# A macaron block on one core: the residual stream is laid out token by partition

## The reference, cut to what matters

```
h = rms_norm(x, g_ffn1_pre)
x = x + 0.5 * rms_norm((silu(h @ w_gate) * (h @ w_up)) @ w_down, g_ffn1_post)      # d_ff = 4096

h = rms_norm(x, g_mix_pre);  proj = h @ w_in      # q,k,v (8 heads x 64), q,k,v,g (4 x 128), two gates (1024 each)
o_sb = stick_breaking_attention(q_sb, k_sb, v_sb)              # strictly causal
o_r  = group_norm(retention(rotary(q_r), rotary(k_r), v_r)) * silu(g_r)
merged = sigmoid(gate_sb) * (o_sb @ w_proj_sb) + sigmoid(gate_ret) * (o_r @ w_proj_ret)
x = x + rms_norm(merged @ w_out, g_mix_post)

h = rms_norm(x, g_ffn2_pre)                                    # then a second FFN like the first
```

## Time and profile before

| | |
|---|---|
| three runs | 1584.85, 1585.07, 1587.95 us |
| span of the profiled execution | 1583.4 us; the page gives no time of its own for that execution beyond the span |
| TensorE busy | 1535.9 us (97%) |
| VectorE, ScalarE, GpSimd busy | 638.3, 495.1, 96.5 us |
| DMA | 138.67 MB, 88 GB/s over the span |
| chain that ended last | PE 93%, DVE 5%, ACT 1%, DMA 1% |

### The profile page before, as it was taken

One profiled execution on the slowest core, in us unless ns is written; L12 is line 12 of the kernel. 1 busy time (PEld: TensorE's weight loads), 2 busy tenths in 40 slices (PEclk: granted clock), 3 DMA queues, 4 the chain that ended last, 5 costly groups with the idle time before them and its releaser, 6 DMA issues.

```text
span 1583.4 us, 17821 instructions
## 1 busy us (share of the span) xinstructions
PE 1535.9 (97%) x6549; PEld 1213.2 (77%) x6549; DVE 638.3 (40%) x753; ACT 495.1 (31%) x689; POOL 96.5 (6%) x145
## 2 busy tenths in 40 slices
PE   6999999999999979999999999899999999999996
PEld 5888888888888767666657887678888888888884
DVE  4433333333333473435545444463333333333334
ACT  4312212222222343445554232332212222222222
POOL 1000000000000040321220000220000000000001
PEclk9999999999999979999999999899999999999997
DMA  6333333333222212111112334133333333322211
GB/s 208 94 106 93 93 106 93 93 102 107 95 93 93 79 53 82 53 53 54 34 34 68 99 86 133 54 93 93 93 101 93 98 94 93 117 94 93 93 40 54
DMA packets 201007, 138.67 MB, mean 88 GB/s; under 512 B 4448, under 2 KB 188816, under 8 KB 200848
## 3 DMA queue, kind: packets, MB, share of 16 engines
q1 hardware_dynamic: 200160, 135.28, 28.7%
q10 hardware_dynamic: 816, 2.98, 0.5%
HBM read 136.14 MB, written 2.10 MB: 87 GB/s over the span
## 4 chain that ended last, share of the span: by engine, by line
PE 93%; DVE 5%; ACT 1%; DMA 1%; issue 0%; ACTq 0%; POOL 0%; DVEq 0%
PE ps L378 28%; PE ps L379 28%; PE ps L380 28%; PE ps L578 2%; DVE h_lo L916 1%; PE ps L555 1%; DVE ys L911 1%; PE ps L503 1%; PE ps L505 1%; PE ps L504 1%; PE ps L542 1%; PE ps L559 1%; PE ps L546 1%; DVE acc L943 1%; DVE w_lo L888 1%; DMA x_tok<-x 1%
## 5 line engine op out<-in xcount | busy, mean ns | idle before, releaser
L378 PE MATMUL ps<-h_hi,w_hi 128*128 128x512 f32 x1312 | 525.0, 400 | 9.7 <-DVE h_lo L916 7.3
L380 PE MATMUL ps<-h_hi,w_lo 128*128 128x512 f32 x1312 | 512.5, 391 | 0.0
L379 PE MATMUL ps<-h_lo,w_hi 128*128 128x512 f32 x1312 | 512.5, 391 | 0.0
L888 DVE TENSOR_TENSOR w_lo<-w_raw,w_hi 128x1024 fp32r<-128x1024 f32 (+1 forms) x260 | 311.4, 1200 | 172.3 <-ACT w_hi L655 164.1
L378 PEld LDWEIGHTS ps<-h_hi,w_hi 128*128 128x128 f32 x1312 | 247.3, 188 | 79.9 <-issue 24.7
L379 PEld LDWEIGHTS ps<-h_lo,w_hi 128*128 128x128 f32 x1312 | 247.4, 189 | 53.0 <-issue 3.4
L380 PEld LDWEIGHTS ps<-h_hi,w_lo 128*128 128x128 f32 x1312 | 247.2, 188 | 52.5
L655 ACT ACTIVATE w_hi<-w_raw 128x1024 fp32r<-128x1024 f32 (+1 forms) x260 | 257.6, 1019 | 32.5 <-PE ps L380 25.2
L380 PE MATMUL ps<-a_hi,w_lo 128*128 128x512 f32 x512 | 202.2, 395 | 0.0
L378 PE MATMUL ps<-a_hi,w_hi 128*128 128x512 f32 x512 | 202.2, 395 | 0.0
L379 PE MATMUL ps<-a_lo,w_hi 128*128 128x512 f32 x512 | 202.2, 395 | 0.0
(11 more groups left out here) (140 smaller groups left out, 998.4 us busy)
## 6 DMA issues: line engine op xcount, KB each, us to landing
w_raw<-w_ffn_gate SPq DMA_DIRECT2D x64, 512.0 KB, 4.0
w_raw<-w_ffn_up SPq DMA_DIRECT2D x64, 512.0 KB, 4.0
w_raw<-w_ffn_down SPq DMA_DIRECT2D x64, 512.0 KB, 3.3
w_raw<-w_in SPq DMA_DIRECT2D x44, 512.0 KB, 3.8
w_raw<-w_out SPq DMA_DIRECT2D x8, 512.0 KB, 3.7
w_raw<-w_proj_sb SPq DMA_DIRECT2D x8, 256.0 KB, 2.6
w_raw<-w_proj_ret SPq DMA_DIRECT2D x8, 256.0 KB, 2.5
out<-x_tok SPq DMA_DIRECT2D x8, 256.0 KB, 2.7
```

The lines of the kernel that those rows point to most:

```text
L378: pe.matmul(ps[:, bank, :], wh, src_hi, start=first, stop=False)
L379: pe.matmul(ps[:, bank, :], wh, src_lo, start=False, stop=False)
L380: return pe.matmul(ps[:, bank, :], wl, src_hi, start=False, stop=last)
L888: dve.tensor_tensor(w_lo[:, slot, 0:cols], w_raw[:, slot, 0:cols], w_hi[:, slot, 0:cols].bitcast(F32), ALU.subtract).then_inc(w_lo_done, 1)
```

## The change

The residual stream is kept as `x_tok`, tokens on partitions (4 tiles, t, of 128 tokens by 1024 features). Each product that is added to it (down, out) is computed with the activations stationary and the weights moving (`row_product`), so a token tile's output is a pair of PSUM banks. Norms are sums along the free axis: ScalarE squares with `accum_out`, a root, a reciprocal on VectorE, and the scale and the gain (loaded broadcast to all partitions, `g_b`) are applied in one operation. h is normalised completely in `xn`, transposed by eight TensorE transposes a tile into PSUM and split to `h_hi` and `h_lo`; so the scaling by `r_all` is gone from the up projections, fills and merge, GpSimd's residual and squares are gone, and so are the transposes at the end. The last four units (`LAST = SLOTS`) of each down projection and of the out projection run token tile by token tile; at the two starts of an FFN the first four up units run in halves of 256 tokens. x and the first tables are loaded in another order.

Core of the diff (same on both FFNs and with like orders on each engine):

```diff
-        a_hi, e = place("a_hi", [P, 2, T], F32R, at=e)
+        a_hi, e = place("a_hi", [P, SLOTS, T], F32R, at=e)
...
+            def row_product(bank, s_hi, s_lo, slot, col, first, last):
+                wh, wl = w_hi[:, slot, col:col + T], w_lo[:, slot, col:col + T]
+                pe.matmul(ps[:, bank, :], s_hi, wh, start=first, stop=False)
+                pe.matmul(ps[:, bank, :], s_hi, wl, start=False, stop=False)
+                return pe.matmul(ps[:, bank, :], s_lo, wh, start=False, stop=last)
...
+            def transposed(n, t):
+                pe.wait_ge(xn_done, TT * n + t + 1)
+                for k in range(KD):
+                    mm = pe.transpose(ps[:, 2 * t + k // 4, tok(k % 4)], xn[:, t % 2, k * P:(k + 1) * P], c(IDENT))
+                mm.then_inc(xt_done, 1)
+            def half_unit(u, j, half):
+                if half == 0:
+                    pe.wait_ge(w_lo_done, u + j + 1)
+                cs = slice(half * 2 * P, (half + 1) * 2 * P)
+                for k in range(KD):
+                    mm = product(j, (j, k * P), h_hi[:, k, cs], h_lo[:, k, cs], k == 0, k == KD - 1, cs)
...
+            def last_down(fi, u0, t):
+                for f in range(NF - LAST, NF):
+                    if t == 0:
+                        pe.wait_ge(w_lo_done, f + u0 + 2 * NF + 1)
+                        pe.wait_ge(a_lo_done, f + NF * fi + 1)
+                    slot = f % SLOTS
+                    for dh in range(2):
+                        mm = row_product(2 * t + dh, a_hi[:, slot, tok(t)], a_lo[:, slot, tok(t)], slot, dh * T, ...)
...
+            last_down(0, U_UP1, 0)          # TensorE, FFN1 to mixing
+            last_down(0, U_UP1, 1)
+            last_down(0, U_UP1, 2)
+            transposed(1, 0)
+            last_down(0, U_UP1, 3)
+            transposed(1, 1)
+            values_sb(0)
+            transposed(1, 2)
+            values_sb(1)
+            transposed(1, 3)
+            values_sb(2)
+            values_sb(3)
...
+            last_out(0)                     # TensorE, mixing to FFN2
+            last_out(1)
+            last_out(2)
+            transposed(2, 0)
+            last_out(3, (0,))
+            transposed(2, 1)
+            last_out(3, (1,))
+            transposed(2, 2)
+            pe.wait_ge(h_lo_done, 2 * TT + 2)
+            half_unit(U_UP2, 0, 0)
+            half_unit(U_UP2, 1, 0)
+            half_unit(U_UP2, 2, 0)
+            transposed(2, 3)
+            half_unit(U_UP2, 3, 0)
+            pe.wait_ge(h_lo_done, 3 * TT)
+            for j in range(4):
+                half_unit(U_UP2, j, 1)
...
+            def y_spread(n, t, last_unit):      # ScalarE; x_spread is the same on x_tok
+                act_eng.activation(junk[:, :], bank_pair(t).rearrange("p b c -> p (b c)"), ACT.Square,
+                                   accum_out=ssq[:, t:t + 1]).then_inc(y_squared, 1)
+                act_eng.wait_ge(y_squared, TT * n + t + 1)
+                act_eng.activation(std[:, t:t + 1], ssq[:, t:t + 1], ACT.Sqrt, bias=cst[:, EPS:EPS + 1], scale=1.0 / D
+                                   ).then_inc(y_std, 1)
...
+            def into_stream(n, t, g, gain_half, halves=1):      # VectorE
+                dve.wait_ge(y_std, TT * n + t + 1)
+                dve.reciprocal(rstd[:, t:t + 1], std[:, t:t + 1]).then_inc(y_rstd, 1)
+                dve.wait_ge(y_rstd, TT * n + t + 1)
+                w = D // halves
+                for i in range(halves):
+                    cs = slice(i * w, (i + 1) * w)
+                    yv = bank_pair(t).rearrange("p b c -> p (b c)")[:, cs]
+                    dve.scalar_tensor_tensor(out=yv, in0=yv, scalar=rstd[:, t:t + 1], in1=g_b[:, G_SLOT[g], cs], ...)
+                    dve.wait_ge(y_scaled, TT * n + t + i + 1)
+                    dve.scalar_tensor_tensor(out=x_tok[:, t, cs], in0=yv, scalar=gain_half, in1=x_tok[:, t, cs], ...)
+            def normalise(n, t, g):
+                ...
+                dve.scalar_tensor_tensor(out=xn[:, t % 2, :], in0=x_tok[:, t, :], scalar=rstd[:, TT + t:TT + t + 1],
+                                         in1=g_b[:, G_SLOT[g], :], op0=ALU.mult, op1=ALU.mult).then_inc(xn_done, 1)
...
+            into_stream(0, 0, G_POST1, 0.5)     # VectorE, FFN1 to mixing
+            normalise(1, 0, G_PRE_MIX)
+            into_stream(0, 1, G_POST1, 0.5)
+            normalise(1, 1, G_PRE_MIX)
+            into_stream(0, 2, G_POST1, 0.5)
+            stream_lo(1, 0)
+            split_u(U_V)
+            normalise(1, 2, G_PRE_MIX)
+            split_u(U_V + 1)
+            split_u(U_V + 2)
+            split_u(U_V + 3)
+            into_stream(0, 3, G_POST1, 0.5)
+            stream_lo(1, 1)
+            normalise(1, 3, G_PRE_MIX)
+            stream_lo(1, 2)
+            stream_lo(1, 3)
...
-                        act_eng.wait_ge(q_scaled, 2 * s + j + 1)
+                        act_eng.wait_ge(unit_done, U_HEADS + f + 1)
```

More of the change, by code:

```diff
@@ L382, in unit @@
-            def unit(u, slot, bank, hi, lo, nk=KD, each_k=None, midway=None):
+                pe.matmul(ps[:, bank, out_cols], wh, src_hi, start=first, stop=False)
+                pe.matmul(ps[:, bank, out_cols], wh, src_lo, start=False, stop=False)
+                return pe.matmul(ps[:, bank, out_cols], wl, src_hi, start=False, stop=last)
+            def row_product(bank, s_hi, s_lo, slot, col, first, last):
[3 more added lines that the diff above has]
+                return pe.matmul(ps[:, bank, :], s_lo, wh, start=False, stop=last)
@@ L384, in unit @@
+            def unit(u, slot, bank, hi, lo, nk=KD):
                 pe.wait_ge(w_lo_done, u + 1)
                 for k in range(nk):
-                    if each_k is not None:
-                        pe.wait_ge(each_k[0], each_k[1] + k + 1)
-                    if midway is not None and k == nk // 2:
-                        midway()
                     last = product(bank, (slot, k * P), hi[:, k, :], lo[:, k, :], k == 0, k == nk - 1)
                 last.then_inc(unit_done, 1)
-            def token_sums(bank, squares, first, last):
-                for j in range(TT):
-                    mm = pe.matmul(ps[:, bank, j:j + 1], squares[:, j * P:(j + 1) * P], c(ONES, 1),
-                                   start=(first and j == 0), stop=last, skip_group_check=True)
-                return mm
@@ L446, in ffn, with down, step @@
                         up(i, j)
-                def down(f, slot, banks, first=False, last=False):
-                    pe.wait_ge(w_lo_done, f + u0 + 2 * NF + 1)
+            def down(fi, u0):
+                ud = u0 + 2 * NF
+                def step(f, slot, tiles=range(TT), first=False):
+                    pe.wait_ge(w_lo_done, f + ud + 1)
                     pe.wait_ge(a_lo_done, f + NF * fi + 1)
-                    for d in banks:
-                        if first and d == 0:
+                    for t in tiles:
+                        if first and t == 0:
@@ L458, in down @@
                     mm.then_inc(unit_done, 1)
-                pe.wait_ge(r_all_ready, 4 * fi + 1)
-                down(0, 0, (4, 5, 6, 7, 0, 1, 2, 3), first=True)
-                with pe.Fori(0, (NF - 3) // SLOTS) as turn:
+                step(0, 0, (2, 3, 0, 1), True)
+                with pe.Fori(0, (NF - SLOTS) // SLOTS - 1) as turn:
                     i = turn * SLOTS + 1
                     for j in range(SLOTS):
-                        down(i + j, (j + 1) % SLOTS, range(KD))
-                for f in range(NF - 3, NF):
-                    down(f, f % SLOTS, Y_ORDER, last=(f == NF - 1))
@@ new lines, in _, with copy_v @@
+            stream_hi(1, 1)
+            x_spread(1, 3)
+            stream_hi(1, 2)
+            stream_hi(1, 3)
+            def copy_v(n, dst, t, bank):
+                if t < TT - 1:
+                    act_eng.wait_ge(v_ready, (TT - 1) * n + t + 1)
+                else:
+                    act_eng.wait_ge(unit_done, U_V + 4 * n + 4)
+                act_eng.activation(dst[:, t, :], ps[:, bank, :], ACT.Copy).then_inc(v_copied, 1)
+            copy_v(0, v_sb, 1, 2)
+            for j in range(4):
+                split_u(U_V + 4 + j)
@@ L1029, in _ @@
[L1029 to L1046 removed]
+                        part(f + 1, (f + 1) % SLOTS)
```

752 lines of the change are left out of this document (341 added, 411 removed).

## The result

The changed kernel takes 1542.31 us (median of 4 runs, 1541.72 to 1543.44) beside 1584.96 for the kernel before on the same chip (1584.72 to 1587.95). The ratio is 0.9726, with a 95% interval of 0.9713 to 0.974. The forecast was 1540, with a range of 1532 to 1555. The span of the profiled execution is 1540.0 us, 43.4 less than before.

A forecast was written before the change was run, and what follows sets the result against it. The prediction took TensorE, busy 1535.9 of 1583.4 us, as the bound. Its terms, −10.4 + 0.8 − 11.3 − 9.4 + 1.7 − 17.0 = −45.6, gave span 1537.8 and time 1539.5, stated as 1540, range 1532 to 1555.

The forecast's parts named there:

- Which buffer moves: Down projections: with weights moving, a matmul steps by 226.7 ns for 233.5, over 1536 matmuls 10.4 us less.
- Rival A: Down projections: the step stays at 233.5 ns although the weights move, time 1550; chance 0.15.
- Four weight pairs within one tile: Last four down units: all weight pairs needed within the first tile's 5.4 us, a_lo late by 0.4 per FFN, +0.8 us.
- The borders: FFN1 to head fills 52.1 us for 63.44, 11.3 less; merge to second up loop 74.2 for 83.60, 9.4 less.
- the block of transposes: Eight transposes per token tile at the borders and the start, priced at 0.207 us each, 1.66 us a tile.
- The half unit: Up unit of 256 columns at an FFN's start: 0.12 us a matmul, 2.9 us each; bound 384 matmuls × 0.107 = +41.
- The wait for tm: Merge to second up loop: out projection begins on tile 3, whose banks are free, so a 0.9 us wait goes.
- The start: Kernel start to up loop: 48.7 us for 47.01, +1.7, with half clock for the first 4 us.
- The end: Last down matmul to kernel end: 8.9 us for 25.71, counted as 17.0 less.
- B: Borders: VectorE becomes the bound, 7.0 against TensorE's 7.1 us a tile; at 15% more, 4 us each, 1548; chance 0.16.
- C: The clock falls around each block of transposes, 2.9 us a fall, +23 at eight amid matmuls, 1563; chance 0.04.
- D: Down and out projections: moving weights read slower while ScalarE and VectorE write them, 95 ns a matmul, +164, 1704; chance 0.03.

The follow-up runs named there:

- aligned_a: The changed kernel with only a_hi and a_lo placed 384 bytes higher, a multiple of 512 bytes from w_hi and w_lo: 1533.83 us.
- before_aligned: The kernel before the change with its buffer region 128 bytes higher and the o buffers 352 lower: 1573.79 us, ratio 0.9924 to before.
- xn_twice: The changed kernel with VectorE making each xn twice at both borders: 1552.39 us.
- transposes_twice: The changed kernel with each of the eight blocks of eight transposes amid matmuls run twice over: 1544.96 us.
- aligned_all: The changed kernel with a, m, o, q and k all moved to a multiple of 512 bytes from the weights: 1533.22 us.
- usual_order: The changed kernel with the last four units of both down projections and the out projection run unit by unit, not token tile by token tile: 1572.41 us.
- whole_units: The changed kernel with the first four up units of both FFNs run whole behind all four tiles' transposes, not in halves: 1557.85 us.
- warm_start: aligned_all with gain and root table loaded earlier, weight unit 0 split between the tiles, and unread transposes in TensorE's pauses: 1527.84 us.

## Why the prediction was right and wrong

*Which buffer moves (forecast -10.4; failed).* The step failed where it concluded "the slow step goes with what moves". The two pairs of rows it rested on differed in three things at once: in what moves, in the bank order, and in where the buffers lie. It checked the bank order and overlooked the addresses; with the operands turned the changed kernel still steps by 232.4 ns. The steps of the earlier trace rows fit the distance of the operands as well, and aligned_a and before_aligned settle it: 226.7 ns in either operand order. Rival A's statement (the step stays) was right to 1 ns; its time was not, because of the next point.

*Four weight pairs within one tile (+0.8; right).* The two waits for a_lo are 0.7 us.

*The borders (-11.3 and -9.4; right in mechanism, 2.8 and 1.0 short).* The mis-sized term is the block of transposes: 0.80 us where 1.66 was put. Over four blocks at each border that is 3.4 us less; the waits took part of it back (1.6 at the first for 1.1 forecast, 1.7 at the second for 1.1), and at the second the out projection steps by 232 ns and not by 227, 1.1 more; 0.7 of that border stays open. The price came from a row at half clock, and the granted clock in it did not tell. The half unit, a width for which one row spoke, takes 2.9 us as put (its bound of 384 matmuls is that of both FFN starts together, one border has 192). VectorE's operations came out as put: 1.29 and 1.22 for the two of into_stream and 1.29 for xn, against 1.24 and 1.3 with its wait.

*The wait for tm.* It is gone. In the kernel before it lies behind the cut at 968.30, so its 0.9 us are part of the second border, in the forecast and in the measurement.

*The start (+1.7; +0.3 measured).* The up loop begins at 47.29 for 48.7. The first half unit came 0.6 later than forecast (the gain landed at 9.6 us and held up the first scaling), the transposes amid the half units took 0.8 and not 1.66 us, and no drain was seen at the two table loads: 1.28 each, the next operation 0.01 us behind. By the drain that the Trainium skill gives ("ScalarE: Activation LUTs", What ACT_TABLE_LOAD costs) the loop would have begun later.

*The end (-17.0; -18.7 measured).* 7.0 us for 8.9: square and root 1.4 for 1.6, reciprocal and the two halves 3.1 for 3.5, and 2.4 from the last write to the end for 3.9, which had been taken from the kernel before. By the prediction's own 8.9 the term was 16.8 and not 17.0.

*The rivals.* B holds in its mechanism and not in its price: VectorE does set the borders' pace (xn_twice), but short by 3.3 us in all and not 4 at each. C is excluded for the changed kernel (transposes_twice), though falls came with longer pauses in aligned_all, xn_twice, usual_order and whole_units. One of the two arguments against it was misread: the 30 transposes at the start ran at the half-clock step of 213 ns and not at the full one, which is 109. (Its ten blocks are twelve: four at the start and eight at the borders.) D is excluded by the changed kernel's step of 232.4 ns, where it wanted 253 and more, and by aligned_a, where the moving weights are read at 226.7 ns while ScalarE and VectorE write them.

So the forecast came out near partly by luck: 9.3 us too much for the down step stand against 7.1 too little for the borders, the start, the heads and the end, of which the transposes at half clock are the largest part.

## What to carry to other kernels

When the same matmul shape steps at two speeds, compare the addresses of the operands before their roles; padding buffers to a multiple of 256 bytes apart costs a few hundred bytes and gave 8.5 to 11.2 us here. Where a product is followed by a norm over its rows, finish its last units tile by tile, so that the chain of one tile has another tile's matmuls beside it; that was 30 of the 43 us, with the clock that holds by it. Take the price of an operation only from rows whose neighbours run at full speed, and from a stretch where the granted clock has already changed once. Short pauses of TensorE in front of heavy work can be filled with matmuls nobody reads, but no more than fit: in warm_start 30 of them delayed the work by 1.4 us.

## What the runs showed of the hardware that was not expected

- A float32r matmul of 512 columns steps by 226.7 ns when its two operands lie a multiple of 256 bytes apart in SBUF, and by 229 to 234 ns at the other distances tried, multiples of 32; at 256 columns no such difference was seen (119.8 and 118.7 ns). Why was not found out.
- Transposes alone bring the engine from 213 to 109 ns a step, and with 12 of them in the pause at the second border the clock held, where it fell for 3.4 us in aligned_all. No two runs differ in these 12 alone, so that they did it is likely and not shown.
- The granted clock in the rows reads 1.00 ahead of its first change in a trace, whatever the engine's speed.
- A square with row sum is two entries on ScalarE, 1.02 to 1.06 us and 0.19 us for reading the sum.
